# A narrow weight tile taken apart: small fp32 products, step sizes with tokens on the partitions, and a first load issued by ScalarE

## The chip, the cores and the metric

The kernel runs on one core of a Trainium2 chip. The core has five engines with a queue each: TensorE (PE, matrix products; its weight loads are shown as PEld), VectorE (DVE), ScalarE (ACT), GpSimd (POOL) and SyncE (SP), which here only issues transfers. The metric is the device time of the launch in microseconds, the median of several runs. Lower is better.

## The reference

The reference is two model blocks on 512 tokens of width 1024. The change touches only the beginning of the first: the input projection and what is made of its two narrowest results, the gate's input of low rank (`gate_lr`, 16 columns) and the raw step sizes (`dt_raw`, 8 columns, one for each head of the state-space mixer).

```python
IN_SIZES = (GLA_QK_WIDTH, GLA_QK_WIDTH, GLA_WIDTH, GLA_GATE_RANK, GLA_WIDTH,      # 256, 256, 512, 16, 512
            SSD_WIDTH, SSD_CONV_DIM, SSD_HEADS)                                    # 512, 768, 8
n = rmsnorm(h, norm_mix_w[i])                  # (512, 1024), w_in: (1024, 2840)
proj = n @ w_in[i]
q, k, v, gate_lr, g_out, z, xbc, dt_raw = split_cols(proj)

# gated linear attention
log_a = jax.nn.log_sigmoid(gate_lr @ w_gate2 + b_gate) / GLA_GATE_NORMALIZER

# state-space mixer, chunks of 128 tokens
xbc = jax.nn.silu(causal_depthwise_conv(xbc, conv_w, conv_b))
dt = jax.nn.softplus(dt_raw + dt_bias)
A = -jnp.exp(a_log)
a_cum = jnp.cumsum(dt * A, axis=2)             # within each chunk
Lmat = jnp.exp(jnp.where(causal, a_cum[l] - a_cum[s], -jnp.inf))
decay_to_end = jnp.exp(a_cum[:, :, -1:] - a_cum)
chunk_decay = jnp.exp(a_cum[:, :, -1])
```

Behind the mixers come an output projection, a layer of product-key experts, and the second block (spatial gating, two wide MLPs, banded attention).

## The kernel before

Activations lie with features on the partitions and tokens along the rows: `hT` is x, turned, in 8 blocks of 128 features by 512 tokens. Every large product is made to nearly fp32 precision out of three products in the format fp32r: both operands are split into a high part and the rest, and `three` (lines 311 to 313) adds high by high and both mixed products in PSUM. For x the parts are `Xh` (ScalarE, `fold_hi`, line 592, which also multiplies with the norm's weight) and `Xl` (VectorE, `fold_lo`, line 597). The norm's root is taken only later: `root_pe` sums the squares (line 525), `spread_pe` spreads the root over the partitions (line 551), and VectorE multiplies each result with it as it leaves PSUM (`scaled`, line 1129).

Weights come as tiles of 128 x 1024 (512 KB): one tile holds 128 output columns for all 1024 features. There are 487, all through one ring of four buffers. `load_w` (line 284, SyncE) loads tile n, `split_hi` (line 292, ScalarE) makes `wh`, `split_lo` (line 300, VectorE or GpSimd) makes `wl`, and TensorE works 24 products of 512 columns with it. The semaphores `s_wd`, `s_wh`, `s_wl`, `s_wuse` count these steps, so the number of a tile also is the count that others wait for. A tile may be loaded when the low part of the tile four before it is made, and split when TensorE is done with that one.

Tile 0 of the projection is called misc. Of its 128 columns only 24 are filled: 8 of `dt_raw` (rows 0 to 7 of the result) and 16 of `gate_lr` (rows 32 to 47); the others are zero. Tiles 1 and 2 are the matrices B and C of the mixer, 3 to 6 its input (all six go through the convolution), 7 to 10 q and k. Then come four tiles for v, four for z, four for the output gate.

The order on each engine is written out by hand in one function per engine and stage; there is no scheduler.

- `in_sp` issues `vec` (all small vectors), the first two blocks of x, tiles 0 to 2, the other blocks by two, tile 3.
- `in_pe` first multiplies `ones` with itself 19 times (line 886). Then it works tiles 0, 1 and 2 together, feature block by feature block as these come in (the first phase; blocks 0 and 1 with tiles 0 and 1 first), then the sums of squares, tile 3, the spreading, tile 4, the two products with `w_gate2` (line 937), tiles 5 to 8, `turn_dt_pe`, tiles 9 and 10, `last_sums_pe`, `turn_b_pe`, and v.
- The step sizes lie with 8 heads on the partitions and 512 tokens in a row (8 x 512). VectorE adds the bias (line 1265), softplus is made of absolute value, exp and ln on ScalarE (lines 1030 to 1046) and a correction on VectorE (lines 1269 to 1282); line 1284 multiplies with -exp(a_log), and four scans (line 1288) sum within the chunks. `turn_dt_pe` (line 726) turns step sizes and sums so that tokens lie on the partitions, and `last_sums_pe` (line 735) spreads the last sum of each chunk. The sums also go to `ac_scratch` in memory, from where they come back spread over the partitions (lines 684, 687, 670).
- Between these steps VectorE evicts and convolves (`xbc_dve`, line 1129; `conv_dve`, line 1144), in the same order in which ScalarE starts the convolutions (`conv_act`, line 969) and ends them (`silu_act`, line 974).

Banks of PSUM are freed by the engine that reads them; `bank_free` makes TensorE wait for it.

## Time and profile before

| | |
|---|---|
| median of 3 runs | 2532.28 us (2531.97 to 2532.74) |
| profiled execution | 2532.24 us |
| its span, first to last instruction | 2530.5 us |
| TensorE busy | 2520.5 us, 100% of the span |
| VectorE, ScalarE, GpSimd busy | 1617.3, 1035.7, 1002.1 us |
| bytes read and written | 442.98 and 42.88 MB |
| products | 13674 instructions |

How to read it: busy time is the time in which at least one instruction of the engine ran. A matrix product in the trace is longer than its distance from the next one, because products are pipelined: with 512 columns a product lasts 0.39 us and the next starts 0.23 us behind it. So distances of starts tell what a product costs, and durations don't. One plain fp32 product is two instructions in the trace (a transpose is one). "Idle before" names what the engine waited for last. The span is shorter than the execution's time by 1.74 us.

### The profile page before, as it was taken

Reading aid. Unit: us, or ns where it says so; the run is one execution under the profiler, and the core shown is the slowest. Engines: PE = TensorE matmul, PEld = TensorE weight load, DVE = VectorE, ACT = ScalarE, POOL = GpSimd, SP = SyncE. Lnnn points to the kernel's source line nnn. Section 1 sums busy time; section 2 is a strip of 40 time slices with the busy share of each in tenths; the row PEclk is TensorE's granted clock in tenths of the full one; section 3 lists DMA queues with packets and bytes.
Section 4 is the critical chain, followed back from the end, with each engine's and each line's share of the span. In section 5 each row is a group of like instructions: output and inputs, shape, how many; then the busy total and the mean of one; then the engine's idle time right before and its main releaser. Section 6 shows DMA issues by size and latency. Waiting matters only on the chain.

```text
span 2530.5 us, 35784 instructions
## 1 busy us (share of the span) xinstructions
PE 2520.5 (100%) x13674; PEld 2196.4 (87%) x13674; DVE 1617.3 (64%) x3033; ACT 1035.7 (41%) x1621; POOL 1002.1 (40%) x545
## 2 busy tenths in 40 slices
PE   9999999999999999999999999999999999999999
PEld 7789899999999988888888888888889877988888
DVE  6746989899999978888888656610216275730112
ACT  6644344444444433333333534522324365542332
POOL 3324344535555523333332054444441424254442
PEclk9999999999999999999999999999999999999999
DMA  4313255789999999999999332223322322232331
GB/s 157 128 59 109 92 154 161 220 271 359 393 404 405 327 325 343 360 349 350 356 345 348 131 113 87 92 92 100 96 96 74 126 84 69 74 117 92 99 100 59
DMA packets 192907, 488.35 MB, mean 193 GB/s; under 512 B 18505, under 2 KB 83929, under 8 KB 192481
## 3 DMA queue, kind: packets, MB, share of 16 engines
q1 hardware_dynamic: 155872, 351.83, 41.6%
q0 software_dynamic: 36864, 134.23, 14.1%
q8 instruction: 109, 1.79, 0.3%
q14 instruction: 62, 0.50, 0.1%
HBM read 442.98 MB, written 42.88 MB: 192 GB/s over the span
## 4 chain that ended last, share of the span: by engine, by line
PE 91%; DVE 5%; DMA 2%; ACT 1%; POOL 1%; issue 1%; SPq 0%; DVEq 0%; ACTq 0%; POOLq 0%
PE ps L311 29%; PE ps L313 28%; PE ps L312 28%; PE ps L1750 1%; DVE wl L300 1%; DMA tmpb<-in_un,idx 1%; DMA rsb<-in_un,idx 1%; PE ps L2771 1%; PE ps L2868 1%; PE ps L1560 1%; PE ps L2831 1%; DVE tmpb L1879 1%; PE ps L525 0%; POOL wl L300 0%; ACT wh L292 0%
## 5 line engine op out<-in xcount | busy, mean ns | idle before, releaser
L292 ACT ACTIVATE wh<-wraw 128x1024 fp32r<-128x1024 f32 x487 | 514.0, 1058 | 1172.3 <-PE ps L313 1162.4
L300 POOL TENSOR_TENSOR wl<-wraw,wh 128x1024 fp32r<-128x1024 f32 x253 | 618.0, 2450 | 940.5 <-ACT wh L292 823.4
L311 PE MATMUL ps<-Xh,wh 128*128 128x384 f32 (+2 forms) x2336 | 828.9, 355 | 2.6 <-POOL wl L300 0.8
L313 PE MATMUL ps<-Xh,wl 128*128 128x384 f32 (+2 forms) x2336 | 817.5, 350 | 0.0
L312 PE MATMUL ps<-Xl,wh 128*128 128x384 f32 (+2 forms) x2336 | 817.2, 350 | 0.0
L311 PEld LDWEIGHTS ps<-Xh,wh 128*128 128x128 f32 x2336 | 439.7, 188 | 46.3 <-issue 5.5
L313 PEld LDWEIGHTS ps<-Xh,wl 128*128 128x128 f32 x2336 | 439.6, 188 | 38.7
L312 PEld LDWEIGHTS ps<-Xl,wh 128*128 128x128 f32 x2336 | 440.2, 188 | 36.2
L300 DVE TENSOR_TENSOR wl<-wraw,wh 128x1024 fp32r<-128x1024 f32 x234 | 286.0, 1223 | 82.2 <-ACT wh L292 78.9
L311 PE MATMUL ps<-wh,Hh 128*128 128x512 f32 x768 | 299.0, 389 | 0.0
L313 PE MATMUL ps<-wh,Hl 128*128 128x512 f32 x768 | 298.8, 389 | 0.0
L312 PE MATMUL ps<-wl,Hh 128*128 128x512 f32 x768 | 298.8, 389 | 0.0
L2165 POOL DMA_INDIRECT vg<-in_v,idx x128 | 163.0, 1274 | 324.4 <-DVE va L2138 288.6
L2646 DVE SCALAR_TENSOR_TENSOR tmpb<-ps,rsb 128x512 f32<-128x512 f32 x64 | 43.9, 689 | 359.2 <-PE ps L313 359.1
L311 PE MATMUL ps<-Fh,wh 128*128 128x512 f32 (+1 forms) x576 | 210.8, 366 | 0.0
L312 PE MATMUL ps<-Fl,wh 128*128 128x512 f32 (+1 forms) x576 | 210.5, 365 | 0.0
L313 PE MATMUL ps<-Fh,wl 128*128 128x512 f32 (+1 forms) x576 | 210.5, 365 | 0.0
L313 PEld LDWEIGHTS ps<-wh,Hl 128*128 128x128 f32 x768 | 144.1, 188 | 29.9
L312 PEld LDWEIGHTS ps<-wl,Hh 128*128 128x128 f32 x768 | 144.2, 188 | 29.9
L311 PEld LDWEIGHTS ps<-wh,Hh 128*128 128x128 f32 x768 | 144.2, 188 | 29.9
L2138 DVE SCALAR_TENSOR_TENSOR va<-vg,hid,va 128x1024 f32<-128x1024 f32 x127 | 162.4, 1279 | 1.6 <-DVE va L2138 0.5
L1897 POOL DMA_INDIRECT tmpb<-in_un,idx x64 | 102.0, 1593 | 109.1 <-DVE hid L1879 99.4
(328 smaller groups left out, 3010.2 us busy)
## 6 DMA issues: line engine op xcount, KB each, us to landing
wraw<-in_uT SPq DMA_DIRECT2D x128, 512.0 KB
wraw<-in_v SPq DMA_DIRECT2D x128, 512.0 KB
wraw<-in_up SPq DMA_DIRECT2D x128, 512.0 KB
gA_scratch<-gl SPq DMA_DIRECT2D x122, 192.0 KB
gl<-gA_scratch SPq DMA_DIRECT2D x122, 192.0 KB
gG_scratch<-gbuf SPq DMA_DIRECT2D x64, 256.0 KB
lg<-gG_scratch SPq DMA_DIRECT2D x64, 256.0 KB
wraw<-in_w_q SPq DMA_DIRECT2D x24, 512.0 KB
```

The source lines that it names most:

```text
L292: act.activation(wh[:, n % 4, :], wraw[:, n % 4, :], ACT.Copy).then_inc(s_wh, 1)
L300: pool.tensor_tensor(wl[:, n % 4, :], wraw[:, n % 4, :], wh[:, n % 4, :].bitcast(F32), ALU.subtract).then_inc(s_wl, 1)
L311: pe.matmul(o, ah, bh, start=start, stop=False)
L312: pe.matmul(o, ah, bl, start=False, stop=False)
L313: return pe.matmul(o, al, bh, start=False, stop=stop)
L1560: mm = pe.matmul(ps[b][:, ts], qb[:, m % 2, ts], kb[:, m, :], start=True, stop=True)
L1750: mm = pe.matmul(ps[b][:, (i % 4) * 128:(i % 4 + 1) * 128], oh[k % 2][0][:, j // 2, :, j % 2], oh[k % 2][1 + w][:, j // 2, :, j % 2], star ...
L1879: dve.tensor_tensor_reduce(out=fetch[f], in0=fetch[f], in1=xrow, scale=1.0, scalar=0.0, op0=ALU.mult, op1=ALU.add, accum_out=hid[:, k:k + ...
L1897: pool.indirect_dma_start(out=fetch[k % nf], out_offset=None, in_=A["un"], in_offset=bass.IndirectOffsetOnAxis(ap=idx[:, k:k + 1], axis=0) ...
L2138: dve.scalar_tensor_tensor(out=va, in0=vg[k % 4], scalar=hid[:, k:k + 1], in1=va, op0=ALU.mult, op1=ALU.add).then_inc(s_va, 1)
L2165: pool.indirect_dma_start(out=vg[k % 4], out_offset=None, in_=A["v"], in_offset=bass.IndirectOffsetOnAxis(ap=idx[:, k:k + 1], axis=0)).the ...
L2646: dve.scalar_tensor_tensor(out=tmpb[:, k % 4, :], in0=ps[bu[m]][:, :], scalar=0.0, in1=RS, op0=ALU.max, op1=ALU.mult).then_inc(s_fe[layer], 1)
```

## The change

Tile 0 goes: `IN_A` becomes -1 and each tile gets the number before its own. The 24 narrow columns come in an array of their own, `w_misc`: 128 partitions x 8 feature blocks x 32 columns (139 KB), with the bias and a_log of the 8 heads behind it, spread over the partitions. It lands in `Ss`, which is free then. GpSimd multiplies it with the norm's weight (`wm`), and `misc_pe` makes 8 plain fp32 products of it with x as loaded, 32 columns each. The product of feature block kc goes to partitions 32 (kc mod 4) on, so four partial results lie in the four quarters of one bank: blocks 0 and 1 inside the first phase, 2 to 7 at its end. The quarters are added by the products that come next: `dt_pe` multiplies the four token chunks of the scaled `misc` with `sel`, four identities of 8 columns one below the other, and `gate_lr_pe` uses `w_gate2` four times below itself.

Step sizes now come out of `dt_pe` with 128 tokens on the partitions and 4 x 8 values in a row (128 x 32), and all steps up to `adt`, the product with -exp(a_log), have this shape. The sums in the chunks become products with the triangle `tri` in `decay_sums_pe`: once for (head, chunk) on the partitions (32 x 128, for memory), once for tokens on the partitions, and one with `ones` for the last sums. `decay_sums_pe` stands behind tile 7 of the old numbers; `turn_dt_pe`, which stood behind 8, and `last_sums_pe` behind 10 go.

The first tile (B's) is loaded by ScalarE as its first instruction and split in two halves. SyncE starts with block 0 of x alone, then `vec`, block 1, tile 1, `w_misc`, tile 2, and two transfers of three blocks. 10 products of `ones` remain of 19. Tiles 1, 2 and 3 of the old numbers make the first phase. Four high parts of weights stand ahead of a silu each on ScalarE, instead of behind the convolution start that follows it.

```diff
-IN_A, IN_V, IN_Z, IN_G, W_OUT, W_Q, W_U, W_V = 0, 11, 15, 19, 23, 31, 47, 175
+IN_A, IN_V, IN_Z, IN_G, W_OUT, W_Q, W_U, W_V = -1, 10, 14, 18, 22, 30, 46, 174
...
+    w2, sel = dg[:, 0:256], dg[:, 256:264]
+    wm = Ss[:, 0, :].rearrange("p (c m) -> p c m", m=32)
+    dtb, alog = Ss[:, 1, 0:8], Ss[:, 1, 8:16]
...
+    y = dtt[:, :, :]
+    X_PARTS = ((0, 1), (1, 2), (2, 5), (5, 8))
+    MISC_FIRST, MISC_REST = (0, 1), (2, 3, 4, 5, 6, 7)
...
     def in_sp(sp):
-        sp.dma_start(vec[:, :], A["vec"]).then_inc(s_vec, 16)
-        for i in range(4):
+        for i, (lo, hi) in enumerate(X_PARTS):
+            sp.dma_start(hT[:, lo:hi, :], xt[:, lo:hi, :]).then_inc(s_x[i], 16)
+            if i == 0:
+                sp.dma_start(vec[:, :], A["vec"]).then_inc(s_vec, 16)
             if i == 1:
-                for n in range(3):
-                    load_w(sp, n)
-            sp.dma_start(hT[:, 2 * i:2 * i + 2, :], xt[:, 2 * i:2 * i + 2, :]).then_inc(s_x[i], 16)
+                load_w(sp, 1)
+                sp.dma_start(Ss[:, 0:2, :].rearrange("p a t -> p (a t)")[:, 0:272], A["w_misc"]).then_inc(s_small, 16)
+                load_w(sp, 2)
...
     def in_pool(pool):
+        pool.wait_ge(s_vec, 16)
+        pool.wait_ge(s_small, 16)
+        mix = vec[:, COLS["mix"]:COLS["mix"] + 8].unsqueeze(2).to_broadcast([128, 8, 32])
+        pool.tensor_tensor(wm, wm, mix, ALU.mult).then_inc(s_const, 1)
         masks_pool(pool)
...
+    def misc_pe(pe, kcs):
+        for kc in kcs:
+            j = 32 * (kc % 4)
+            pe.wait_ge(s_x[X_PART[kc]], 16)
+            mm = pe.matmul(ps[B_INA[0]][j:j + 32, :], wm[:, kc, :], hT[:, kc, :], start=kc < 4, stop=kc >= 4)
+        return mm
+    def dt_pe(pe):
+        pe.wait_ge(s_in, 1)
+        pe.wait_ge(s_const, C_SEL)
+        bank_free(pe, 6)
+        for tc in range(4):
+            mm = pe.matmul(ps[6][:, tc * 8:tc * 8 + 8], misc[:, tc * 128:(tc + 1) * 128], sel, start=True, stop=True)
+        mm.then_inc(s_mp, 1)
+    def gate_lr_pe(pe):
+        pe.wait_ge(s_small, 32)
+        for m in range(2):
+            b = 7 if m == 0 else 5
+            bank_free(pe, b)
+            pe.matmul(ps[b][:, :], w2[:, m * 128:(m + 1) * 128], misc, start=True, stop=True).then_inc(s_gp, 1)
+    def decay_sums_pe(pe):
+        pe.wait_ge(s_dt, 8)
+        pe.wait_ge(s_const, C_TRI)
+        b, by_tok = AUX["sp"], adt.rearrange("p (h c) -> p c h", c=4)
+        bank_free(pe, b)
+        pe.matmul(ps[b][0:32, 128:256], adt, tri[:, :], start=True, stop=True)
+        pe.matmul(ps[b][:, 0:32], tri[:, :], by_tok, start=True, stop=True).then_inc(s_sp, 1)
+        b = AUX["acl"]
+        bank_free(pe, b)
+        pe.matmul(ps[b][:, 0:32], ones[:, :], by_tok, start=True, stop=True).then_inc(s_sp, 1)
...
-        for i in range(19):
+        for i in range(10):
...
-        for c, gs in ((0, (0, 1)), (1, (0, 1)), (0, (2,)), (1, (2,)), *((c, (0, 1, 2)) for c in range(2, 8))):
+        for c, gs in ((0, (1,)), (1, (1,)), (0, ()), (0, (2,)), (1, (2,)), (0, (3,)), (1, (3,)), *((c, (1, 2, 3)) for c in range(2, 8))):
             pe.wait_ge(*XL["in"][c])
+            if not gs:
+                pe.wait_ge(s_const, C_WM)
+                misc_pe(pe, MISC_FIRST)
...
+        misc_pe(pe, MISC_REST).then_inc(s_mp, 1)
...
         root_pe(pe, "in", 5)
-        project(3)
+        project(4)
         spread_pe(pe, "in", 6, (s_kept, 1))
-        project(4)
-        pe.wait_ge(s_w2, 16)
...
         project(5)
+        dt_pe(pe)
+        gate_lr_pe(pe)
         project(6)
         project(7)
+        decay_sums_pe(pe)
         project(8)
-        turn_dt_pe(pe)
         project(9)
         project(10)
-        last_sums_pe(pe)
...
     def in_act(act):
+        act.dma_start(wraw[:, 0, :], tiles[0]).then_inc(s_wd[0], 16)
...
             if c == 0:
-                split_hi(act, 0)
+                act.wait_ge(s_wd[0], 16)
+                act.activation(wh[:, 0, 0:512], wraw[:, 0, 0:512], ACT.Copy).then_inc(s_w0, 1)
+                act.activation(wh[:, 0, 512:1024], wraw[:, 0, 512:1024], ACT.Copy).then_inc(s_wh, 1)
+            if c == 1:
                 split_hi(act, 1)
...
     def in_dve(dve):
...
-        dve.wait_ge(s_in, 1)
-        dve.tensor_scalar(y, y, col("dtb", 0, 0, 8), None, ALU.add).then_inc(s_dt, 1)
         xbc_dve(dve, 0)
         xbc_dve(dve, 1)
+        dve.wait_ge(s_mp, 2)
+        dve.tensor_tensor(y, ps[6][:, 0:32].rearrange("p (c h) -> p c h", h=8),
+                          dtb.unsqueeze(1).to_broadcast([128, 4, 8]), ALU.add).then_inc(s_dt, 1)
...
-        dve.tensor_scalar(z, y, ea1[:, 0:1], -1.0, ALU.mult, ALU.mult).then_inc(s_dt, 1)
-        for c in range(4):
-            dve.tensor_tensor_scan(acT[:, cs], ones[0:8, :], z[:, cs], 0.0, ALU.mult, ALU.add).then_inc(s_dt, 1)
+        dve.scalar_tensor_tensor(out=adt.rearrange("p (h c) -> p c h", c=4), in0=y, scalar=-1.0,
+                                 in1=ea1[:, :].unsqueeze(1).to_broadcast([128, 4, 8]), op0=ALU.mult,
+                                 op1=ALU.mult).then_inc(s_dt, 1)
```

How the instructions stand. TensorE at the start of the program, before; a name `ps<-Xh,wh` is output and operands, and the semaphores that an instruction waits for stand in brackets:

```order
L886 MATMUL ps<-ones 128x128 [waits s_const]
L886 MATMUL ps<-ones 128x128 x18
L311 MATMUL ps<-Xh,wh 128x512 [waits s_wl,s_xld]
L312 MATMUL ps<-Xl,wh 128x512
L313 MATMUL ps<-Xh,wl 128x512
L311 MATMUL ps<-Xh,wh 128x512 [waits s_wl]
```

The same place in the changed kernel, whose lines stand 3 lower here; L743 is `misc_pe`:

```order
L926 MATMUL ps<-ones 128x128 [waits s_const]
L926 MATMUL ps<-ones 128x128 x9
L314 MATMUL ps<-Xh,wh 128x512 [waits s_w0,s_xld]
L315 MATMUL ps<-Xl,wh 128x512
L316 MATMUL ps<-Xh,wl 128x512
L314 MATMUL ps<-Xh,wh 128x512 [waits s_w0,s_xld]
L315 MATMUL ps<-Xl,wh 128x512
L316 MATMUL ps<-Xh,wl 128x512
L743 MATMUL ps<-hT,Ss 32x512 [waits s_x0,s_const,s_xld]
L743 MATMUL ps<-hT,Ss 32x512 [waits s_x1]
L314 MATMUL ps<-Xh,wh 128x512 [waits s_wl,s_xld]
```

The second group of three waits for half a tile and block 1 instead of a second tile, and two narrow products stand third. TensorE behind tile 5 in the changed kernel, where before only the two products of `gate_lr` stood, one tile earlier:

```order
L316 MATMUL ps<-Xh,wl 128x512
L751 MATMUL ps<-sqdg,kendt 128x8 [waits s_kept,s_const,s_in]
L751 MATMUL ps<-sqdg,kendt 128x8 x3
L760 MATMUL ps<-kendt,sqdg 128x512 [waits s_small]
L760 MATMUL ps<-kendt,sqdg 128x512 [waits s_root]
L314 MATMUL ps<-Xh,wh 128x512 [waits s_wl,s_in]
```

`dt_pe` (L751; `kendt` holds `misc`, `sqdg` holds `sel` and `w_gate2`) moved in ahead of `gate_lr_pe` (L760). ScalarE at the start of the changed kernel, where before the table load stood first and the tile was split in one piece:

```order
L1047 DMA wraw<-in_w_in 128x1024
L565 ACT_TABLE_LOAD
L565 ACTIVATE warmb<-epsc 128x1 [waits s_const]
L595 ACTIVATE Xh<-hT,vec 128x512 [waits s_x0,s_vec]
L1056 ACTIVATE wh<-wraw 128x512 [waits s_wd0]
L1057 ACTIVATE wh<-wraw 128x512
L595 ACTIVATE Xh<-hT,vec 128x512 [waits s_x1]
```

The two halves of the tile now stand between the first two blocks of x, and the second tile behind them.

## Rows read from the trace of the kernel before

**Rows 1.** The page: busy time, chain by engine, one of its groups.
```profile
PE 2520.5 (100%) x13674; PEld 2196.4 (87%) x13674; DVE 1617.3 (64%) x3033; ACT 1035.7 (41%) x1621; POOL 1002.1 (40%) x545
...
PE 91%; DVE 5%; DMA 2%; ACT 1%; POOL 1%; issue 1%; SPq 0%; DVEq 0%; ACTq 0%; POOLq 0%
...
L300 POOL TENSOR_TENSOR wl<-wraw,wh 128x1024 fp32r<-128x1024 f32 x253 | 618.0, 2450 | 940.5 <-ACT wh L292 823.4
```

**Rows 2.** The list of waits of TensorE, longest first: total, times, longest.
```profile
PE ps L886 <- POOL ones L608: 1.7, 1, 1.7
```

**Rows 3.** The timeline up to 12 us: start, duration, engine, what, idle before.
```profile
0.82 0.39 SPq L673 DMA_DIRECT2D vec<-in_vec  x1
...
1.26 0.42 SPq L678 DMA_DIRECT2D hT<-in_xT  x1
...
1.74 6.82 PE L886 MATMUL ps<-ones 128*128 128x128 f32 x38 [1.74 <-POOL ones L608]
...
5.15 0.72 ACT L592 ACTIVATE Xh<-hT,vec 128x512 fp32r<-128x512 f32 x1 [2.84 <-DMA hT<-in_xT]
...
6.37 1.06 ACT L292 ACTIVATE wh<-wraw 128x1024 fp32r<-128x1024 f32 x1 [0.50 <-DMA wraw<-in_w_in]
7.46 2.50 DVE L300 TENSOR_TENSOR wl<-wraw,wh 128x1024 fp32r<-128x1024 f32 x2 [0.69 <-ACT wh L292]
...
8.83 0.47 PE L311 MATMUL ps<-Xh,wh 128*128 128x512 f32 x1 [0.27 <-DVE wl L300]
...
10.01 0.50 PE L311 MATMUL ps<-Xh,wh 128*128 128x512 f32 x1 [0.24 <-DVE wl L300]
```

**Rows 4.** Windows: a stretch of all engines, then two of line L886 alone.
```profile
5.00:8.80 3.80, 3.56 (x25) 3.37 (x24) 2.04 (x3) 2.93 (x4) 0.00 (x0) 1.00 1.02 412
...
5.70:6.70 1.00, 1.00 (x7) 1.00 (x6) 1.00 1.01 414
6.70:7.70 1.00, 1.00 (x11) 1.00 (x10) 1.00 1.02 418
```

**Rows 5.** The timeline of TensorE at the end of the first phase.
```profile
25.82 0.95 PE L525 MATMUL ps<-ones,sqdg 128*128 128x1 f32 x8
26.63 0.49 PE L311 MATMUL ps<-Xh,wh 128*128 128x512 f32 x1
...
32.22 0.60 PE L551 MATMUL ps<-ident,rst 128*128 128x128 f32 x4
```

**Rows 6.** The timeline of TensorE: products that lie beside each other.
```profile
95.05 1.52 PE L777 MATMUL ps<-vt 128*64 128x256 f32 x12
96.50 1.09 PE L812 MATMUL ps<-ident,GE 128*128 128x128 f32 x8
...
131.50 0.67 PE L841 MATMUL ps<-vt,kendt 64*64 64x128 f32 x16
```

**Rows 7.** The timeline of TensorE: the second product of gate_lr.
```profile
39.18 1.02 PE L937 MATMUL ps<-kendt,sqdg 16*128 16x512 f32 x2
40.13 0.50 PE L311 MATMUL ps<-Xh,wh 128*128 128x512 f32 x1
```

**Rows 8.** The timeline of TensorE around turn_dt_pe and turn_b_pe.
```profile
61.80 0.39 PE L313 MATMUL ps<-Xh,wl 128*128 128x512 f32 x1
...
63.05 0.50 PE L311 MATMUL ps<-Xh,wh 128*128 128x512 f32 x1 [0.28 <-DVE tmpb L1129]
...
74.23 0.52 PE L744 MATMUL ps<-ident,xs 128*128 128x128 f32 x3
```

**Rows 9.** The timelines of ScalarE and VectorE: the chain of the step sizes.
```profile
34.30 1.99 DVE L1265 TENSOR_SCALAR kendt<-kendt,vec 8x512 f32<-8x512 f32 x1
...
36.98 1.28 ACT L1032 ACT_TABLE_LOAD   x1
...
45.99 0.63 ACT L1046 ACTIVATE GE<-kT 8x512 f32<-8x512 f32 x1
...
53.09 2.50 DVE L1284 TENSOR_SCALAR GE<-kendt,ea 8x512 f32<-8x512 f32 x1
```

More of the change, by code:

```diff
@@ L690, in in_sp @@
             lt_load(sp, h)
-        for n in range(13, 19):
+        for n in range(12, 18):
             load_w(sp, n)
@@ L915, in within_g @@
                 spread_pe(pe, f"s{g}", AUX[f"r{g}"], (s_xt, XTK["out", 2 * g + 5] + 1))
[L918 removed]
+        for c, gs in ((0, (1,)), (1, (1,)), (0, ()), (0, (2,)), (1, (2,)), (0, (3,)), (1, (3,)), *((c, (1, 2, 3)) for c in range(2, 8))):
             pe.wait_ge(*XL["in"][c])
+            if not gs:
+                pe.wait_ge(s_const, C_WM)
+                misc_pe(pe, MISC_FIRST)
             for g in gs:
[L921 to L923 removed]
+                if g == 1 and c < 4:
+                    pe.wait_ge(s_w0, 2)
+                else:
+                    pe.wait_ge(s_wl, IN_A + g + 1)
+                w, cs = IN_A + g, slice(c * 128, c * 128 + 128)
+                mm = three(pe, ps[B_INA[g]][:, :], wh[:, w, cs], wl[:, w, cs], Xh[:, c, :], Xl[:, c, :], c == 0, c == 7)
                 if c == 7:
                     mm.then_inc(s_wuse, 1)
[L926 removed]
+                    freed[B_INA[g]] = done_in(g)
+        misc_pe(pe, MISC_REST).then_inc(s_mp, 1)
+        freed[B_INA[0]] = done_in(0)
         pe.wait_ge(s_const, C_ONES)
         root_pe(pe, "in", 5)
[L929 removed]
+        project(4)
         spread_pe(pe, "in", 6, (s_kept, 1))
[L931 to L939 removed]
         project(5)
+        dt_pe(pe)
+        gate_lr_pe(pe)
         project(6)
         project(7)
+        decay_sums_pe(pe)
         project(8)
[L944 removed]
         project(9)
         project(10)
[L947 removed]
         turn_b_pe(pe)
@@ L1024, in in_act @@
             sum_square(act, "in", c, hT[:, c, :])
-        for n in range(4, 7):
+        for n in range(4, 6):
             split_hi(act, n)
         root_act(act, "in", 5, 1.0 / 1024)
-        split_hi(act, 7)
+        split_hi(act, 6)
         act.wait_ge(s_dt, 1)
@@ L3128, in _layout @@
     q, k, vv, gl, go, z, xbc, dt = (w[:, at[i]:at[i + 1]] for i in range(8))
-    misc = np.zeros((1024, 128), np.float32)
+    misc = np.zeros((1024, 32), np.float32)
     misc[:, 0:8] = dt
-    misc[:, 32:48] = gl
-    a["w_in"] = np.concatenate([_tiles(np.concatenate([misc, xbc[:, 512:], xbc[:, :512], q, k], 1)), _tiles_tok(vv),
+    misc[:, 8:24] = gl
+    rows = np.concatenate([v["ssd_dt_bias"][0], v["ssd_a_log"][0]])
+    a["w_misc"] = np.ascontiguousarray(np.concatenate([misc.reshape(8, 128, 32).transpose(1, 0, 2).reshape(128, 256),
+                                                       np.broadcast_to(rows[None], (128, 16))], 1))
+    a["w_in"] = np.concatenate([_tiles(np.concatenate([xbc[:, 512:], xbc[:, :512], q, k], 1)), _tiles_tok(vv),
                                 _tiles(z), _tiles_tok(go)], 0)
```

152 lines of the change are left out of this document (69 added, 83 removed).

## The prediction

> **What bounds the kernel now.** I read the page first. It shows TensorE busy for 2520.5 of 2530.5 us, and 91% of the chain that ended last on it [rows 1]. The list of waits by engine, longest first, then shows how little TensorE waits: at the top stand 1.7 us for the operand of its very first products [rows 2]. So a microsecond of TensorE's work that goes, or by which its dense work starts sooner, should be a microsecond of the time, provided that nothing else becomes late. All edits lie in the first 75 us, and I read these in the timeline. The profiled execution took 2532.24 us, 1.74 more than its span; the median of the runs shown is 2532.28. I sum against 2532.24.
>
> In the timeline the reader is to see three pieces. First the start: TensorE only turns `ones` from 1.74 us, and its first useful product starts at 8.83 [rows 3]. What it waited for is the first tile: `vec`, then two blocks of x, then the tile, all issued by SyncE; ScalarE starts on x at 5.15 and on the tile at 6.37, VectorE on its low part at 7.46, and the product starts 0.12 us after that part ends (two of them in 2.50 us, so 1.25 each). Second, dense products up to 25.82, then tile after tile [rows 5]. Third, one stall, at `turn_dt_pe`: the last product before it starts at 61.80 and the next one at 63.05, with 0.28 us put down to an eviction by VectorE [rows 8].
>
> **The start.** Removed ahead of the first product: one of the two x blocks (256 of 512 KB), and part of what SyncE issues ahead of the tile, at about 0.4 us each (0.39 and 0.42 in [rows 3]). Transfers run at 412 GB/s once they flow [rows 4]. Before, 70 + 512 + 512 = 1094 KB had to land with the tile. Now its own 512 KB, 256 KB of x and 70 KB of `vec` are needed, with part of the next block beside them, as two queues share the transfer engines: some 950 KB. That is 150 KB less, 0.35 us. The first large transfer is also asked for 0.44 us earlier (0.82 against 1.26). Together about 0.8 us: the tile is there at 5.55 instead of 6.35.
> The split in halves: ScalarE's 1.06 us and VectorE's 1.25 us before the first product become about 0.6 and 0.7 (half the columns and a fixed part), 1.0 us less. So the first useful product would start at 8.83 - 0.8 - 1.0 = 7.0; I take 6.9. Bounds: 7.9 (only the halves bring something) and 6.2 (the tile also comes ahead of x and `vec`).
> Behind it a gap stands, before as well: the second group started at 10.01, although the first was 0.69 us of work, so 0.5 us were lost [rows 3]. Now VectorE has the second half (0.7) and the low part of x's block 1 (0.75) to make between the first and the second group: a gap of 0.75. Net of the start: 8.83 - 6.9 less 0.25, so -1.7 us.
> The issue by ScalarE itself saves the tile SyncE's queue and no more, by this sum. "Initiating DMAs on multiple engines concurrently will only save the time on the sequencer it takes to initiate the DMA", says the Trainium skill (DMA: Bandwidth & Descriptors, Issuing engines are not separate DMA queues). Without the halves and the smaller blocks the start would by that rule gain some 0.4 to 0.8 us, an estimate. No row of before has a transfer issued by ScalarE.
>
> **The narrow columns.** Removed: tile 0, 24 products of 512 columns. From 26.63 to 32.22 a tile takes 5.59 us with 0.1 for the change from another kind of product [rows 5]: 5.5 us, 0.229 each. Added: 8 plain fp32 products of 512 columns with 32 stationary columns, to partitions 0, 32, 64 and 96 of one bank. The price of one by itself is in `gate_lr`'s old pair: the second stands from 39.18 to the next start at 40.13, 0.95 us for two instructions, 0.1 of it the change of kind, so 0.427 per instruction and 0.85 per product [rows 7].
> One after another the eight would cost 6.8 us, more than the tile. The question is whether products to different partitions run beside each other. Two rows say so. `ssd_states_pe` has 12 instructions of 256 columns, alternately to partitions 0 and 64: they would take 12 x 0.213 = 2.56 us, and take 1.45 (95.05 to 96.50). `gla_states_pe` has 16 of 128 columns over four quarters of the array: 16 x 0.107 = 1.71 us, and the row shows 0.67 with its tail [rows 6]. So two column blocks run at once, and quarters do too. No row shows four streams of 128 partitions each. I take full overlap: the first pair 0.85; of the other six four at once and then two, 1.7; with four changes of kind of 0.1 it is 2.95 us. Bounds: in pairs only, 0.85 more (3.8); one after another, 7.2. Against 5.5 that is -2.55, -1.7 or +1.7 us; the nearest row is that of column blocks with 128 partitions, which overlap fully, so I keep -2.55.
> The Trainium skill (TensorE: Matmul & The Clock Gate, Measured speedup vs the span model) gives 2.38 times for three products side by side with 32 columns each, not 3. By it the six products would take 6 x 0.85 / 2.38 = 2.15 us as an estimate, 0.45 more than I take.
> `wm` is scaled by GpSimd: 256 columns, about a quarter of the 2.45 us of its low part of 1024 [rows 1], 0.6 us. `w_misc` lands behind some 1750 KB, near 7 us, so `wm` is ready by 7.9; TensorE comes to it behind two groups, at 6.9 + 0.75 + 1.4 = 9.0. That hides it. From 9.0 on each microsecond would be one of TensorE.
>
> **The step sizes.** Removed from TensorE: `turn_dt_pe` with its stall, 61.80 + 0.23 to 63.05, 1.0 us; `last_sums_pe`, two short instructions just ahead of `turn_b_pe` at 74.23, 0.15 [rows 8]. Added: `dt_pe`, 8 instructions with a full stationary block and few columns, like the column sums of squares, whose 8 stand from 25.82 to 26.63, 0.8 us [rows 5]; `decay_sums_pe`, two instructions of 128 columns (0.2) and four short ones (0.4), with the change 0.7. `gate_lr` costs the same with 128 partitions as with 16. Net +0.35 us. Bounds 0 and +0.7.
> On VectorE the operations on 8 x 512 become small ones on 128 x 32; the first, with its wait, was 1.99 us and the scaling by `ea` 2.50 [rows 9]. VectorE was what TensorE waited for at 63.05, so this stall should not come back.
> The new waits: `dt_pe` waits for `misc`, which VectorE has scaled by 36 and TensorE needs at 39. VectorE's bias waits for `dt_pe`; ScalarE stands at `s_dt` until then, and behind it in its queue stand the exp, two convolution starts, a high part and the gate's activations. `decay_sums_pe` waits for `s_dt` 8, and behind it in TensorE's queue is project(8). By my times the first phase ends at 6.9 + 0.75 + 72 x 0.229 + 2.95 = 27.1, `dt_pe` (after 0.8 of sums, two tiles, 0.35 of spreading and itself) at 40.1, project(7) (after 1.8 of `gate_lr` and two tiles) at 52.9. From 40.1 on: bias and absolute value 0.4; from the table load at 36.98 to the Ln at 45.99 ScalarE took 9.0 us, now 8.6 with two passes short; then 2.3 for the Ln, VectorE's small steps and an eviction between them: 51.4. So it comes 1.5 us early.
>
> **Sum.** -1.7 - 2.55 + 0.35 = -3.9, so 2532.24 - 3.9 = 2528.3 us. Everything behind 75 us should move as a whole, since TensorE sets it. Every other edit (tile numbers, semaphores, high parts ahead of the silus, 10 warming products) I cost at nothing: what it moves is ready microseconds ahead of TensorE, which still has some eleven tiles of products in this stretch to hide it.
>
> **The rivals.** *The clock rises late.* TensorE's first products went at half rate: 7 instructions of 128 columns in the microsecond up to 6.70 (1.2 GHz) and 11 in the next (2.4 GHz) [rows 4]. So the clock rose near 6.7, after 4.9 us without a pause. Now the ten warming products are 20 instructions of 0.213 us, over by 6.0, and a pause of 0.9 us follows, then a gap. If the clock rises only 4.9 us after the dense work resumes at 8.3, at about 13, 5.5 us of products run at 1.2 GHz and 2.7 us are lost: 2531.0. If it rises halfway, about 1.2 us: 2529.5. For it speaks the pause; against it that most of the stretch up to the old rise is still busy.
> *The overlap is in pairs*: 2529.2. *There is none*: +4.25, so 2532.6, no change by measurement; this needs the eight to take over 6.85 us.
> *The step-size chain takes the place of the stall*, and the kernel is slower. Place: TensorE before `decay_sums_pe`. Before, the chain from the bias to the scaling took 21.3 us (34.30 to 55.59) [rows 9]. If it stays that long, it ends at 61.4 instead of 52.9 and TensorE waits 8.5 us: 2536.8. It costs from 12.8 us of length on and makes the kernel slower than before from 16.7. For it: ScalarE works in order and stands still until the step sizes come, some 4 us later than before. Against it: a good part of the 21 us was VectorE's own large operations.
> *More comes at the start than I take* (product at 6.2, hardly a gap): 2527.0.
>
> **How the numbers follow.** Forecast as worked out 0.42; clock late 0.2 (both prices); pairs only 0.12; no overlap 0.03; chain late 0.05; better start 0.18. A measurement of this kernel tells some 0.2%, 5.1 us, from no change, so faster by more means below 2527.2: the better start and the lower edge of the forecast, 0.25 in all. Slower by more needs over 2537.3: 0.02 of the chain's chance and 0.01 of the clock's and the overlap's together. The rest, 0.72, is within 0.2%. The range has the better start below and the clock's full price above: 2526.2 to 2531.0.
>
> **What would show it.** The first useful product near 6.9 and the second group near 8.3; the six products of `misc` within 1.8 us; the column sums of squares at 27.1 (before, the same tiles were done at 31.3: 25.82 and one tile more); no idle time of TensorE before `decay_sums_pe`; `turn_b_pe` near 70.3 instead of 74.23. The forecast is wrong if the instructions of `misc` start 0.43 us apart one by one, if products of 512 columns stand 0.43 us apart behind 7 us, or if TensorE idles between 39 and 60 us.

## The result and the profile after

The changed kernel takes 2540.5 us (median of 8 runs, 2539.18 to 2541.68), the kernel before 2532.39 us beside it (8 runs, 2531.97 to 2533.79). The ratio is 1.0031, with a 95% interval of 1.0021 to 1.0042: it is 8.1 us slower, 0.3%, slower by the prediction's own bound of 0.2%. The forecast was 2528.3 us, with a range of 2526.2 to 2531.0; the time lies outside, on the other side of the kernel before. The profiled execution took 2541.68 us, 1.78 more than its span.

These lines of the page answer to [rows 1].

```profile
PE 2521.6 (99%) x13652; PEld 2194.0 (86%) x13652; DVE 1614.2 (64%) x3030; ACT 1033.0 (41%) x1621; POOL 1002.1 (39%) x548
...
PE 96%; DVE 1%; ACT 1%; POOL 1%; issue 0%; DMA 0%; SPq 0%; DVEq 0%; ACTq 0%; POOLq 0%
```

TensorE's share of the chain rose from 91% to 96%, although the kernel is slower. So the share of the chain is no measure of what was gained; the list of waits is. Three new rows of it (line and releaser, total, times, longest); the first row of before [rows 2] stands unchanged among them, with 1.7 us:

```profile
PE ps L771 <- DVE tmpb L1169: 5.5, 1, 5.5
...
PE ps L1603 <- issue: 1.6, 1, 1.6
PE ps L314 <- DVE kendt L1169: 1.5, 1, 1.5
```

There are 5.5 us ahead of L771 (`decay_sums_pe`) and 1.5 us ahead of a product of L314 that waits for `kendt`. The 1.6 us at L1603, released by nothing that the profile shows, were between 0.2 and 1.6 in the profiles of this study that list them, and I leave them out.

**The start.** The timeline of all engines, as in [rows 3]: start, duration, engine, line, what, and the idle time before it.

```profile
0.81 0.41 ACTq L1047 DMA_DIRECT2D wraw<-in_w_in  x1
...
1.74 4.64 PE L926 MATMUL ps<-ones 128*128 128x128 f32 x20 [1.74 <-POOL ones L611]
...
5.47 0.72 ACT L595 ACTIVATE Xh<-hT,vec 128x512 fp32r<-128x512 f32 x1 [2.72 <-DMA vec<-in_vec]
6.10 0.61 ACT L1056 ACTIVATE wh<-wraw 128x512 fp32r<-128x512 f32 x1
...
7.01 0.69 DVE L1292 TENSOR_TENSOR wl<-wraw,wh 128x512 fp32r<-128x512 f32 x1
...
7.84 0.77 PE L314 MATMUL ps<-Xh,wh 128*128 128x512 f32 x1 [1.46 <-DVE wl L1292]
...
8.41 0.63 PE L315 MATMUL ps<-Xl,wh 128*128 128x512 f32 x1
...
10.67 1.92 PE L743 MATMUL ps<-hT,Ss 128*32 128x512 f32 x4
...
12.52 0.80 PE L314 MATMUL ps<-Xh,wh 128*128 128x512 f32 x1
...
13.97 0.43 PE L314 MATMUL ps<-Xh,wh 128*128 128x512 f32 x1
```

ScalarE's transfer is asked for at 0.81, and the half tile is worked on at 6.10, but ScalarE came to it from the x block at 5.47, for which it had waited 2.72 us. VectorE made the low part of that x block first (6.34 to 7.09) and came to the tile's low part at 7.01, 0.3 us behind the high part. The first useful product stands at 7.84 (8.83 before, 6.9 forecast). Then the products start 0.43 us apart (8.41 to 8.83 and on) instead of 0.23, and the pair of `misc` takes from 10.67 to 12.52, 1.85 us. At 13.97 the duration falls to 0.43, and from there the products stand 0.23 apart. So, by the distances, the array went at the lower of its two levels, 1.2 GHz, up to 13.9 us. The column of the granted clock shows 1.00 in this stretch, so here this rests on the distances alone; in the profile of the bank experiment below, the column shows 0.50.

**The rest, up to 84 us.** TensorE's timeline at five places. They are the six products of `misc` with the sums of squares behind them, the first product of project(5), `dt_pe`, `decay_sums_pe` with the products behind it, and `turn_b_pe`.

```profile
28.39 1.91 PE L743 MATMUL ps<-hT,Ss 128*32 128x512 f32 x12
30.23 1.05 PE L528 MATMUL ps<-ones,sqdg 128*128 128x1 f32 x8
...
38.82 0.50 PE L314 MATMUL ps<-Xh,wh 128*128 128x512 f32 x1 [1.51 <-DVE kendt L1169]
...
44.40 0.95 PE L751 MATMUL ps<-sqdg,kendt 128*128 128x8 f32 x8
...
63.62 0.60 PE L771 MATMUL ps<-tri,GE 128*32 128x128 f32 x2 [5.52 <-DVE tmpb L1169]
...
65.03 0.77 PE L314 MATMUL ps<-Xh,wh 128*128 128x512 f32 x1
...
68.59 0.42 PE L316 MATMUL ps<-Xh,wl 128*128 128x512 f32 x1
...
83.15 0.38 PE L784 MATMUL ps<-ident,xs 128*128 128x128 f32 x2
```

The six products take 28.39 to 30.23, 1.84 us for twelve instructions. Project(5) waits 1.51 us at 38.82. Behind project(7) TensorE waits 5.52 us, until 63.62. Then the products stand 0.43 us apart again, up to 68.59. `turn_b_pe` starts at 83.15 instead of 74.23 [rows 8]: 8.9 us. At `ssd_states_pe` it is 8.2 us (103.21 instead of 95.05 [rows 6]). The profiled executions differ by 9.4 us in the end, with the 1.6 us at L1603 in it, and the medians by 8.1. So nearly all of the loss stands ahead of `turn_b_pe`.

VectorE's timeline: the bias of the step sizes, the last operation of their chain, the three operations of `conv_dve(1)`, and the scaling of `xbc` 3 that empties bank 4.

```profile
45.38 0.19 DVE L1312 TENSOR_TENSOR dtt<-ps,Ss 128x32 f32<-128x32 f32 x1 [5.42 <-PE ps L751]
...
56.30 0.22 DVE L1331 SCALAR_TENSOR_TENSOR GE<-dtt,ea 128x32 f32<-128x32 f32 x1
56.41 6.28 DVE L1184 SCALAR_TENSOR_TENSOR tmpb<-tmpb,vec 128x511 f32<-128x511 f32 x3
62.78 0.69 DVE L1169 TENSOR_TENSOR tmpb<-ps,rsb 128x512 f32<-128x512 f32 x1
```

GpSimd's timeline beside it, two low parts:

```profile
56.78 5.35 POOL L303 TENSOR_TENSOR wl<-wraw,wh 128x1024 fp32r<-128x1024 f32 x2 [4.65 <-ACT wh L295]
```

The operations on `tmpb` from 56 to 63 us, by line: count, shortest, median and longest in ns.

```profile
L1184 DVE SCALAR_TENSOR_TENSOR tmpb<-tmpb,vec x3: 746/2724/2739, 56.4 to 60.0; 128x511 f32<-128x511 f32 x1, 128x510 f32<-128x510 f32 x1, 128x509 f32<-128x509 f32 x1
```

The step sizes were ready at 56.52, 1.4 us ahead of TensorE. What TensorE waited for is the last row of VectorE: the scaling at 62.78 to 63.47, which empties bank 4. `decay_sums_pe` writes bank 4. It stood in VectorE's queue behind a convolution (and waits for it by `s_conv` too, since it writes into the buffer that this one reads), whose first operation took 746 ns and whose other two took 2724 and 2739 ns, while GpSimd made low parts from 56.78 to 62.13.

Last, windows of TensorE's granted clock behind the wait: the stretch, busy time of each engine, then the clock as a share of full speed (PEclk).

```profile
58.00:64.00 6.00, 0.48 (x3) 0.18 (x2) 5.34 (x3) 4.54 (x6) 4.14 (x2) 0.82 0.01 3
64.00:66.00 2.00, 2.00 (x8) 1.69 (x7) 1.14 (x4) 0.26 (x1) 0.81 (x1) 0.50 0.01 2
66.00:68.00 2.00, 2.00 (x6) 1.58 (x5) 2.00 (x1) 0.00 (x0) 2.00 (x1) 0.50 0.15 39
...
70.00:72.00 2.00, 2.00 (x10) 1.68 (x9) 1.93 (x4) 0.00 (x0) 0.00 (x0) 1.00 1.01 213
```

The clock stands at 0.50 from 64 to 68 us, and at full speed again behind 70. TensorE had done only 0.48 us of work in the six microseconds before. The sums took 1.41 us (63.62 to 65.03) instead of some 0.77, and the eight products from 65.03 to 68.59 cost 3.56 us instead of 1.83. So the wait of 5.5 us brought 2.4 us more.

### The profile page after: what moved, and what is told of

The parts are those of the page before. It is cut to its first block, busy times and chain, and to the rows that moved or that the text cites. A ratio compares the mean times of both kernels' runs of the same rounds, so it can differ in the third digit from the quotient of the medians.

```text
span 2539.9 us, 35743 instructions
## 1 busy us (share of the span) xinstructions
PE 2521.6 (99%) x13652; PEld 2194.0 (86%) x13652; DVE 1614.2 (64%) x3030; ACT 1033.0 (41%) x1621; POOL 1002.1 (39%) x548
## 4 chain that ended last, share of the span: by engine, by line
PE 96%; DVE 1%; ACT 1%; POOL 1%; issue 0%; DMA 0%; SPq 0%; DVEq 0%; ACTq 0%; POOLq 0%
PE ps L314 30%; PE ps L315 30%; PE ps L316 30%; PE ps L1793 2%; PE ps L2814 1%; PE ps L2911 1%; PE ps L1603 1%; PE ps L2874 1%; PE ps L528 0%; POOL wl L303 0%; POOL Xl L587 0%; ACT wh L295 0%; PE ps L2299 0%; DVE tmpb L1184 0%; PE ps L554 0%
## 5 line engine op out<-in xcount | busy, mean ns | idle before, releaser
L314 PE MATMUL ps<-Xh,wh 128*128 128x512 f32 (+2 forms) x2328 | 827.6, 356 | 4.8 <-DVE kendt L1169 1.5
L316 PE MATMUL ps<-Xh,wl 128*128 128x512 f32 (+2 forms) x2328 | 815.7, 350 | 0.0
L315 PE MATMUL ps<-Xl,wh 128*128 128x512 f32 (+2 forms) x2328 | 815.5, 350 | 0.0
L314 PEld LDWEIGHTS ps<-Xh,wh 128*128 128x128 f32 x2328 | 439.2, 189 | 49.5 <-issue 6.2
L314 PE MATMUL ps<-wh,Hh 128*128 128x512 f32 x768 | 299.0, 389 | 0.0
L314 PE MATMUL ps<-Fh,wh 128*128 128x512 f32 (+1 forms) x576 | 210.8, 366 | 0.0
L314 PEld LDWEIGHTS ps<-wh,Hh 128*128 128x128 f32 x768 | 144.2, 188 | 29.9
```

The source lines that it names most:

```text
L314: pe.matmul(o, ah, bh, start=start, stop=False)
L315: pe.matmul(o, ah, bl, start=False, stop=False)
L316: return pe.matmul(o, al, bh, start=False, stop=stop)
```

## The experiments

The theory after the result: the work of ScalarE and VectorE that begins with `dt_pe` now begins some 8 us later against TensorE, and evictions stand behind it in their queues. TensorE then waits for a bank, not for the step sizes. The rival: the chain of the step sizes is itself too long. All kernels are the changed one with the edit shown, and each is compared with the kernel before on the same chip.

**The decay sums in another bank.**

```diff
-        b, by_tok = AUX["sp"], ...
+        b, by_tok = 6, ...
```
(and the two places that read the result)

> The chunk sums go to bank 6, which the bias of the step sizes has freed long before, instead of bank 4. Theory A: TensorE's wait of 5.5 us before the sums was for bank 4, which VectorE's eviction of tile g4 frees only at 63.5 us, not for the step sizes, which were ready at 56.5. Then there is no wait before the sums (TensorE comes at 57.9), but the next eviction in VectorE's queue holds project(9): a wait of some 2.6 us. With 2.9 us less waiting, and up to 1.6 us less at the low clock behind the pause: 2536.0 to 2537.6 (changed kernel: 2540.5). Rival: the step sizes' own chain set the wait; then nothing changes, 2540.5, and 5.5 us stand before the sums as before.

2540.43 us (7 runs), the kernel before 2532.54; ratio 1.0030 (1.0019 to 1.0042): nothing gained. TensorE's timeline:

```profile
57.25 0.41 PE L771 MATMUL ps<-tri,GE 128*32 128x128 f32 x2
...
70.04 0.79 PE L314 MATMUL ps<-Xh,wh 128*128 128x512 f32 x1 [6.26 <-DVE tmpb L1169]
```

The sums start at 57.25 without a wait. So the step sizes were not late, and the wait was for bank 4. But the next reader of a bank takes it over: project(9) waits 6.26 us for the scaling of `xbc` 4, which stands behind the next convolution. I had expected 2.6 us there. The wait belongs to VectorE's late queue, not to one bank. This run's windows show the clock at the start in numbers too:

```profile
8.00:10.00 2.00, 1.75 (x5) 1.19 (x6) 1.65 (x3) 1.17 (x2) 1.17 (x3) 0.72 0.97 305
10.00:12.00 2.00, 2.00 (x6) 0.19 (x5) 1.62 (x2) 0.95 (x1) 1.81 (x5) 0.50 1.04 399
```

The first three products of this run (7.91, 8.21, 8.44) stand at the distances of the full clock; then the clock falls, to 0.50 from 10 to 12 us. In the changed kernel's own profile the same column shows 1.00 between 8 and 14 us, although its products stand 0.43 us apart; there I go by the products.

**The low parts held back.** GpSimd makes the low part of tile 8 only when VectorE has scaled `xbc` 3, and that of tile 9 behind it.

```diff
         for n in range(4, 10):
+            if n == 8:
+                pool.wait_ge(s_in, 5)
             split_lo(pool, n)
```

> GpSimd makes the low part of tile 8 only when VectorE has evicted g4, so it does not work beside VectorE's second convolution. Theory A: that convolution took 6.3 us instead of 2.3 because GpSimd's low parts ran at the same time; held back, it takes 2.3, the eviction is done at 59.4, the wait before the sums shrinks from 5.5 to 1.5 us and the clock does not fall: about 2535. Rival: the convolution is long for another reason; then the wait stays and the late low parts add some 2 us at project(9): 2541 to 2543.

2537.27 us (10 runs), ratio 1.0018 (1.0008 to 1.0027): 3.2 us less than the changed kernel. VectorE's timeline, two convolutions:

```profile
55.46 2.31 DVE L1186 SCALAR_TENSOR_TENSOR tmpb<-tmpb,vec 128x511 f32<-128x511 f32 x3
...
59.77 7.38 DVE L1186 SCALAR_TENSOR_TENSOR tmpb<-tmpb,vec 128x511 f32<-128x511 f32 x3
```

With nothing on GpSimd beside it `conv_dve(1)` takes 2.31 us instead of 6.28, and the wait at the sums is 1.6 us instead of 5.5. But the next convolution takes 7.38 us under the delayed low parts, and project(9) waits 2.8 us. Behind the first of these waits (1.56 us) the products go on at the full clock; behind the second they stand 0.43 us apart from 69.53 to 72.09, which is a part of why only 3.2 us were gained where some 5.5 were expected. Both operands of these operations, and of GpSimd's, lie in SBUF. The Trainium skill (SBUF — State Buffer, Who interferes with whom) says that a VectorE instruction with two SBUF inputs contends with a GpSimd instruction that reads SBUF, and calls the port pair that they share an exclusive lock. The trace agrees: the two operations that lie beside a low part of some 2.4 us took 2724 and 2739 ns, 2 us more than the 746 of the first.

**The spreading inside a tile.** `spread_pe` goes into project(4), so that `misc` is scaled before project(5) needs its bank.

```diff
-        project(4)
-        spread_pe(pe, "in", 6, (s_kept, 1))
+        pe_linear(pe, IN_A, [4], B_INA, None, done_in,
+                  each=lambda m, kc: spread_pe(...) if kc == 2 else None)
```

> The spreading of the root stands inside project(4), behind its third feature block, as against behind the tile. Theory A: the wait of 1.5 us at project(5) was for misc being scaled out of bank 0, which hangs on the spreading just ahead of it; it goes, and dt_pe and everything hung on it come 1.7 us earlier as TensorE does, so that the wait at the sums stays 5.5: 2538.8. Rival: the chain to the sums doesn't start at dt_pe but at something that does not move, and takes the 1.7 us back there: 2540.5.

2538.02 us (10 runs), ratio 1.0021 (1.0012 to 1.0031). The wait of 1.5 us is gone from the list, and the 5.5 us ahead of L771 are still there. The gain of 2.5 us is more than the wait removed; the sums of squares started at 28.77 in this profile, 1.5 us sooner with the same start, so part of it is scatter.

**Sixteen warming products instead of ten.**

```diff
-        for i in range(10):
+        for i in range(16):
```

> 16 warming products instead of 10, over at about 7.6 us by the distances of before, so that TensorE has no pause before its first useful product at 7.8. Theory A: the clock rose only at 13.9 us because of the pause from 6.1 to 7.8; without it, it rises near 6.7 as before, the products in between take 0.23 us each and the first phase ends 1.9 us sooner (the low parts bound it): 2538.6, with the wait at the sums unchanged. Rival: the clock's rise doesn't hang on the pause; then 2540.5.

2539.26 us (10 runs), ratio 1.0026 (1.0017 to 1.0036), 1.2 us less. TensorE's timeline:

```profile
1.75 6.00 PE L926 MATMUL ps<-ones 128*128 128x128 f32 x32 [1.75 <-POOL ones L611]
8.09 0.47 PE L314 MATMUL ps<-Xh,wh 128*128 128x512 f32 x1 [0.34 <-DVE wl L1292]
...
10.57 1.05 PE L743 MATMUL ps<-hT,Ss 128*32 128x512 f32 x4
11.55 0.50 PE L314 MATMUL ps<-Xh,wh 128*128 128x512 f32 x1
```

The warming products now end at 7.75. The pause before the first useful product is 0.34 us, and the products stand 0.23 apart from the first on; `misc`'s pair takes 0.98 us instead of 1.85. The sums of squares start at 28.58 instead of 30.23. So the low clock at the start comes from the shorter warming-up. Both profiles with sixteen products go at the full clock from the first product on. The edit changes two things at once, and this run does not tell them apart: the pause is shorter, and the warming products go on past 6.7 us, where the clock rose before [rows 4], while the ten are over at 6.38. What it costs is less sure. In the seven other profiles of this study with ten warming products and the same first transfers the sums start at 28.77 to 29.49, sooner than in the execution shown above. In five of them the first products are slow as there; in two (the bank's and that of the early `dt_pe`) they go at the full clock and it falls to 0.50 only behind them. Against them the sixteen gain 0.2 to 0.9 us, and by the medians 1.2.

**`dt_pe` and `gate_lr` ahead of project(5)**, with the spreading inside the tile.

```diff
-        project(5)
         dt_pe(pe)
         gate_lr_pe(pe)
+        project(5)
```

> With the spreading inside project(4), dt_pe and the two products of gate_lr stand ahead of project(5) instead of behind it, so the step sizes start some 6 us sooner against TensorE's tiles. Theory A (VectorE's queue of evictions hangs on the step sizes, and TensorE on the evictions): the bias comes at 36.5 us, the eviction of g4 at 54.5 even with the stretched convolution, and TensorE comes to the sums at 54.5; hardly a wait there nor at project(9), no fall of the clock, turn_b_pe near 72.5 (80.0 with the spreading alone, 74.2 before): about 2531. Rival: GpSimd's low parts stretch VectorE's work wherever it stands, and 3 to 5 us of waiting stay at project(9): 2534 to 2536.

2531.0 us (10 runs), the kernel before 2532.33; ratio 0.9995 (0.9986 to 1.0004): 9.5 us less than the changed kernel, and no difference from the one before. VectorE's timeline:

```profile
37.46 0.19 DVE L1312 TENSOR_TENSOR dtt<-ps,Ss 128x32 f32<-128x32 f32 x1 [1.63 <-PE ps L751]
...
48.37 0.21 DVE L1331 SCALAR_TENSOR_TENSOR GE<-dtt,ea 128x32 f32<-128x32 f32 x1
48.48 6.36 DVE L1184 SCALAR_TENSOR_TENSOR tmpb<-tmpb,vec 128x511 f32<-128x511 f32 x3
```

And TensorE's, the sums:

```profile
55.77 0.38 PE L771 MATMUL ps<-tri,GE 128*32 128x128 f32 x2 [0.16 <-DVE tmpb L1169]
```

The chain is as long as before (11.1 us from the start of its first to the end of its last operation, as in the changed kernel). The convolution behind it is stretched to 6.36 us just the same. But all of it stands 8 us earlier, and of the wait of 5.52 us 0.16 is left. Then the clock does not fall either. This experiment decides for the theory that the place of `dt_pe` on TensorE sets the wait, and not the length of the chain.

**All four together:** spreading inside the tile, `dt_pe` early, bank 6, sixteen warming products.

> All four mends: spreading inside project(4), dt_pe and gate_lr ahead of project(5), chunk sums in bank 6, 16 warming products. Theory A: the gains add where they don't share a wait, so 1.3 us less than dt_early by the warm start and no wait at the sums: about 2529.5, some 3 us faster than the kernel before. Rival: bank 6 lets GpSimd's later low parts start sooner beside VectorE's convolutions, the wait moves to project(9) as it did with the bank alone: 2533 or more.

2529.53 us (11 runs, 2528.13 to 2530.76), the kernel before 2532.33; ratio 0.9988 (0.9979 to 0.9997). This version beats both kernels, by 2.8 and by 11 us; the 2.8 us (0.1%) are clear of noise, but below the prediction's own bound of 0.2%. The top of its list of waits of TensorE:

```profile
PE ps L926 <- POOL ones L611: 1.7, 1, 1.7
PE ps L314 <- POOL wl L303: 0.8, 3, 0.3
```

Every other row is 0.5 us or less. The sums of squares stand at 27.89 and `turn_b_pe` at 71.23.

**Another order of the column blocks.** It makes two neighbours in the order share a column block.

```diff
-MISC_REST = (0, 1), (2, 3, 4, 5, 6, 7)
+MISC_REST = (0, 1), (4, 5, 2, 6, 3, 7)
```

> The last six products of misc in the order 4, 5, 2, 6, 3, 7 instead of 2 to 7, so that 2 and 6 and then 3 and 7, which go to the same quarter, follow each other directly. Theory A (products to different quarters run beside each other, those to one quarter don't, and none overtakes another): three rounds of 0.85 instead of two, 2.7 us from the first to the sums of squares instead of 1.84. Rival: the array picks products whose quarter is free out of the queue; then 1.84 stays.

One run, 2540.24 us. TensorE's timeline:

```profile
27.32 1.93 PE L743 MATMUL ps<-hT,Ss 128*32 128x512 f32 x12
29.18 1.05 PE L528 MATMUL ps<-ones,sqdg 128*128 128x1 f32 x8
```

1.86 us instead of 1.84, in one profile. My expectation of 2.7 was wrong: a product that waits for its column block does not hold back the ones behind it in a way that costs anything here.

**The first tile issued by SyncE.**

```diff
-        act.dma_start(wraw[:, 0, :], tiles[0]).then_inc(s_wd[0], 16)
...
                 sp.dma_start(vec[:, :], A["vec"]).then_inc(s_vec, 16)
+                load_w(sp, 0)
```

> The first tile is issued by SyncE, behind vec and ahead of x's block 1, instead of by ScalarE as its first instruction; all else as in the changed kernel. Theory A (the bytes ahead of the tile and the halves decide, and the issue by ScalarE is worth a queue's issue time): x's block 0 and vec land sooner, as they no longer share with the tile, the tile lands within 0.5 us of where it did, and the first useful product stays at 7.6 to 8.3 us (7.84). Rival: the issue by ScalarE is what brings the start forward; then it goes back to 8.8 or later.

One run, 2540.96 us. The timeline of all engines:

```profile
3.72 0.72 ACT L595 ACTIVATE Xh<-hT,vec 128x512 fp32r<-128x512 f32 x1 [1.41 <-DMA vec<-in_vec]
...
6.73 0.63 ACT L1056 ACTIVATE wh<-wraw 128x512 fp32r<-128x512 f32 x1 [2.29 <-DMA wraw<-in_w_in]
...
8.23 0.77 PE L314 MATMUL ps<-Xh,wh 128*128 128x512 f32 x1 [1.85 <-DVE wl L1292]
```

Issued by SyncE behind `vec`, the half tile is worked on at 6.73 instead of 6.10 and the first product starts at 8.23 instead of 7.84. Against the other profiles with ScalarE's issue and ten warming products, where the first product starts between 7.80 and 8.10, the issue by ScalarE is worth 0.1 to 0.4 us, by this one profile. It has a price: `vec` and the first x block are worked on at 3.72 here and at 5.47 with ScalarE's transfer beside them. `vec` took 2.4 us from issue to landing here and 4.2 there, which fits a tile that moves beside it.

**The high parts back behind the convolution starts**, as in the kernel before.

```diff
         for i in range(6):
-            if i < 4:
-                split_hi(act, 9 + i)
             silu_act(act, i)
             if i < 4:
                 conv_act(act, i + 2)
+                split_hi(act, 9 + i)
```

> Of the changed kernel, one part undone: ScalarE makes the four high parts behind the convolution starts again, as in the kernel before, not ahead of the silus. Theory A (GpSimd's low parts beside VectorE's second convolution make half of the wait): only one low part instead of two falls into the convolution, which takes some 4.2 us instead of 6.3; the wait before the sums is 3.4 instead of 5.5 us: 2538.4. Rival: the order of the high parts doesn't matter, since the convolution is late anyway: 2540.5.

2538.27 us (10 runs), the kernel before 2532.22; ratio 1.0024 (1.0015 to 1.0034), 2.2 us less. The wait, from the list:

```profile
PE ps L771 <- DVE tmpb L1168: 3.5, 1, 3.5
```

It fell from 5.5 to 3.5 us. In this kernel only one low part (55.60 to 58.19) falls into the convolution, the next starts at 59.40, and `conv_dve(1)` takes 4.30 us (55.22 to 59.52). So an edit that I had costed at nothing costs 2 us. The clock falls behind this wait too: from 62 to 64 us it stands at 0.50.

**The wait filled with products.** 24 products of `ones` ahead of the decay sums, into a free bank.

```diff
     def decay_sums_pe(pe):
+        bank_free(pe, 6)
+        for i in range(24):
+            pe.matmul(ps[6][:, 0:128], ones[:, :], ones[:, :], start=True, stop=True)
```

> The wait before the chunk sums is filled with 24 products of ones (5.2 us at the full clock), whose results nothing reads. Theory A (the clock falls because TensorE stands still for 5.5 us, and the fall costs by itself): the wait for bank 4 ends where it did, but the clock stays at its full level, the nine or so products behind it go at 0.23 instead of 0.43 us, and the time falls by 1.6 to 2 us: 2538.7. Rival: the clock's fall is hidden behind VectorE's evictions, which hold project(9) anyway: 2540.5.

2538.6 us (10 runs), the kernel before 2532.22; ratio 1.0024 (1.0014 to 1.0034). TensorE's timeline, and a window of all engines with the clock:

```profile
56.90 5.52 PE L769 MATMUL ps<-ones 128*128 128x128 f32 x48
62.59 0.38 PE L774 MATMUL ps<-tri,GE 128*32 128x128 f32 x2 [0.18 <-DVE tmpb L1172]
...
63.37 0.48 PE L314 MATMUL ps<-Xh,wh 128*128 128x512 f32 x1
```

```profile
64.00:66.00 2.00, 2.00 (x11) 1.63 (x10) 1.96 (x2) 0.00 (x0) 2.00 (x1) 1.00 0.03 8
```

The sums come no earlier for it, since bank 4 is still what they need. But they take 0.78 us instead of 1.41, and the clock stays at 1.00. From the sums to `turn_b_pe` it is 17.25 us (62.59 to 79.84) instead of 19.53, 2.3 less: the price of the fall, measured. Not all of it reaches the end. A new wait stands behind `turn_b_pe`, for VectorE's next eviction:

```profile
82.51 0.50 PE L314 MATMUL ps<-wh,Xh 128*128 128x512 f32 x1 [1.48 <-DVE kT L1172]
```

From the sums of squares to `ssd_states_pe` it is 72.47 us (29.19 to 101.66) instead of 72.98 (30.23 to 103.21), so some 0.5 us of the 2.3 is left there. The medians differ by 1.9; how much of that is the clock's and how much is the scatter of the start stays open.

## Why the prediction was wrong, point by point

**The step that failed** is the one on the new waits: "`decay_sums_pe` waits for `s_dt` 8 ... So it comes 1.5 us early", and before it "so this stall should not come back". The first half was right: the chain took 11.1 us from the bias (45.38) to its end (56.52) where I had 11.3, and it came 1.4 us early against TensorE. What it left out is the second wait of the same function. `decay_sums_pe` also waits for its bank, and who frees that is VectorE with the scaling of `xbc` 3, which stands behind the chain and behind a convolution. I named what is queued behind ScalarE's and TensorE's waits and not what is queued on VectorE behind the chain. The bank experiment shows the cause, and that another bank is no cure; the early `dt_pe` shows the root, the order on TensorE. VectorE's side of it was argued from the queue: the scaling can't go ahead of that convolution, since it waits for it, and whether the last steps of the chain would do better behind both was not tried.

**The edits costed at nothing.** "What it moves is ready microseconds ahead of TensorE" fell twice. The earlier high parts release GpSimd's low parts into the convolution: 2 us of the wait. The ten warming products end 1.46 us before the first product and before 6.7 us, where the clock rose in the kernel before, and the first products run in part at the lower level.

**Project(5).** I had `misc` scaled "by 36" and needed "at 39" by `dt_pe`. It was scaled at 38.77, some 3 us later, as the whole start was. But project(5), which stands directly behind the spreading, needs the bank that `misc` is scaled from. That is a wait of 1.5 us that no step of mine spoke of.

**The start.** 7.84 instead of 6.9: the x block waited for `vec` until 5.47, because ScalarE's tile shares the transfers; I had let everything be there at 5.55 and gave ScalarE no queue of its own ahead of the tile. That is 0.55 of the 0.9 us (6.10 instead of 5.55). The other 0.3 us is VectorE, which made the x block's low part ahead of the tile's (7.01 instead of 6.71).

**What held.** The narrow columns: 1.84 us for six products, 1.7 and a change of kind forecast, so four streams beside each other. The rival "in pairs" (2.55) is refuted. The Trainium skill's 2.38 times (TensorE: Matmul & The Clock Gate, Measured speedup vs the span model), by which I had estimated 2.15 us, is given there for three products side by side; these are four and then two, at 5.1 / 1.84 = 2.8 times, and the measurement decides. The pair alone, at full clock, took 0.98 us (10.57 to 11.55) for 0.85 and a change. `dt_pe` took 0.80 us (44.40 to 45.20), the sums 0.77 at full clock for 0.7. Each of these pieces costs what it was forecast at. The version with all four mends, at 2529.53, fits that, 2.8 us faster than the kernel before where 3.9 were forecast, but it is another kernel than the one predicted.

**The rivals.** "The clock rises late" came true beside it: at 13.97 where I had "about 13", and 2.2 us of loss in the profiled execution where I had 2.7 (in the seven other profiles 0.8 to 1.4, near my price for a rise halfway). I gave it 0.2 and it should have had more than a half, since all that spoke against it was that TensorE would be mostly busy. "The step-size chain takes the place of the stall" had the right place, TensorE before `decay_sums_pe`, and near the right price (8.5 us; 5.5 and 2.4 were seen), for the wrong reason, and I gave it 0.05.

**The account**, at the start of the decay sums and up to `turn_b_pe`, in microseconds behind the forecast: 0.9 for the first product and 2.2 for the clock behind it (30.23 instead of 27.1 at the sums of squares), 1.5 at project(5), 5.5 at the decay sums, 2.4 for the second fall of the clock. That is 12.5 of 12.85 (83.15 instead of 70.3). The profiled execution was the longest of the eight; the median stands 12.2 behind the forecast, which the smaller price of the start's clock in other executions fits.

**What stays open.** From profile to profile of kernels with the same ten warming products the sums of squares begin up to 1.5 us apart (30.23 in the changed kernel, 28.77 with the spreading inside the tile), with the stretch in which the clock is low. Why that stretch is longer in one execution than in another was not settled, so differences of 1 us between two medians are not put down to an edit here. Nor was it tried why the order of the column blocks does not matter.

## What to carry to other kernels

When work moves to another engine's queue or begins later, list every semaphore that the next reader waits for, the one that frees its bank among them, and follow each back through the queue of the engine that gives it. What hangs on a small result is decided by where its producer stands on the busiest engine: moving two short steps of TensorE ahead of one tile was worth 7 us here. Here a warming-up of TensorE that lasted nearly until the first useful product kept the full clock, and one that ended 1.46 us before it did not. A wait in the middle can cost its length and then the clock.
